# Taking the sparse steps out of the beats in which the gates are spread, and dividing the one-hots anew

## Chip, core and metric

The kernel runs on one core of a Trainium2 chip. The metric is the device time of one launch, in microseconds; before the change it is 4021.94 us, the median of three runs (4019.43 to 4031.22).

## The reference

A decoder trunk of two layers on 512 tokens of width 1024, all in float32. Each layer adds four mixers' outputs to the residual `h`, and then a product-key expert feed-forward; a last RMSNorm follows. The change touches the expert part alone:

```python
q = (xt @ wq).reshape(t, PEER_HEADS, 2, PEER_KEY_DIM)
sc = jnp.einsum('thcd,hcnd->thcn', q, keys)
s1, i1 = lax.top_k(sc[:, :, 0], PEER_TOPK)
s2, i2 = lax.top_k(sc[:, :, 1], PEER_TOPK)
...
top, pos = lax.top_k(cand, PEER_TOPK)
eidx = jnp.take_along_axis(cidx, pos, axis=-1)
gate = jax.nn.softmax(top, axis=-1)
...
act = jax.nn.gelu(jnp.einsum('td,tkd->tk', xb, u[ib]))
return jnp.einsum('tk,tkd->td', gb * act, v[ib])
```

Each token has 128 picks (8 heads of 16) out of 16384 experts. A pick costs a dot product with the expert's row of `u`, a GELU, a product with its gate, and the expert's row of `v` times that, added to the token.

## The kernel before, in words

Per layer the program runs the mixers, the output projection, then `peer`. `peer` normalises and transposes, computes the queries and ranks the keys, and calls `experts` (lines 1727 to 2004), which works on four chunks of 128 tokens in two ways at once.

**The sparse half.** Tokens 0 to 255 (chunks 0 and 1) gather their experts' rows. One step is one pick of 128 tokens. `gather(n)` on GpSimd (L1795) issues an indirect DMA that brings 128 rows of 2048 floats (a row of `u` and a row of `v`) into one of 7 slots. `dot(n)` on VectorE (L1958) multiplies the `u` half with the tokens and sums; ScalarE takes the GELU of two dots at a time (L1889); `add_row(m)` on VectorE (L1966, L1970), four steps behind (`LAG`), adds the `v` half times its coefficient to `h`. Gather n+3 is issued in the beat of step n and waits for add_row(n-4), which frees its slot. There are 256 steps in a layer.

**The dense half.** Tokens 256 to 511 (chunks 2 and 3) are multiplied with all experts, 128 tiles of 128. `with_u(j)` on TensorE (L1848) makes the tile's activations for 256 tokens, ScalarE takes the GELU (L1895), `gate_tile(j)` on VectorE (L1978) multiplies with the tile's gates, which are zero where a token did not pick the expert, and `with_v(j)` (L1859) adds the tile's output into four PSUM banks over all tiles. The `u` and `v` tiles are loaded by SyncE's queue through rings of four each (L1759, L1765). At most 22 activated tiles are held; 20 `u` tiles are run ahead.

**The gates of the dense half** have to be spread from (first key, second key, gate) triples to a table of 128 x 128 experts for each token. A quad is four tokens; there are 64. For each token one one-hot row over the first key carries the gate (`hot1`: iota equal to the pick, times the gate) and one over the second key does not (`hot2`). VectorE makes two of the four `hot1` of a quad (L1950), GpSimd the other two (L1805). ScalarE makes all four `hot2` with a Square for each (L1903) and one Relu over the four (L1907). TensorE multiplies `hot2` by `hot1` (`spread_quad`, L1837), ScalarE copies the result from PSUM (`copy_quad`, L1915), and after every fourth quad stores it to HBM (L1919). Both `hot` buffers and the PSUM banks are held for two quads, so the one-hots of quad q wait for the spread of quad q-2. After the last store SyncE loads the gates back, eight tiles at a time (L1770).

**The order** is written by hand in beats; each engine runs its own loop over the same 212 beats, and the engines meet only in semaphores. VectorE chooses the picks of chunk 0 before beat 0, and in 14 pieces each those of chunk 2 (from beat 0), chunk 3 (from beat 14) and chunk 1 (from beat 84): `choose_chunk`. Quad q is in beat 16+q, so quads fill beats 16 to 79. `u` tiles 0 to 19 are one in three beats up to beat 59. From beat 84 on (`TILES_AT`) each beat is one tile: `with_u` for tile 20 and on, and `gate_tile` and `with_v`. `steps_until(beat)` says how many sparse steps have been issued before a beat: one step in three beats, two in three after beat 28 (`chosen`), four in beats 80 to 83, and the rest evenly over the 128 tiles. Evaluated for the kernel before it gives 5 at beat 16, 43 at beat 80, 47 at beat 84 and 256 at the end: 1.633 steps a tile.

Of the kernel before, what the change touches and what calls it, by code (L numbers as in the profile page):

```python
# [17 lines left out]
ALU = mybir.AluOpType  # L18
# [43 lines left out]
@contextmanager  # L62
def stage(nc, *names):

    with ExitStack() as held:
        sems = {n: held.enter_context(nc.semaphore(n)) for n in names}
        with nc.Block() as block:  # L67
            yield block, sems
        for s in sems.values():
            nc.sync.sem_clear(s)  # L70
        nc.all_engine_barrier()
# [1446 lines left out]
CHOOSE_AT = {2: 0, 3: 14, 1: 84}  # L1518
PIECES = 14
# [3 lines left out]
QUADS_AT = 16  # L1523
TILES_AT = 84
# [2 lines left out]

def steps_until(beat):

    chosen = CHOOSE_AT[3] + PIECES  # L1530
    if beat <= TILES_AT - 4:
        return max(beat, 0) // 3 + max(beat - chosen, 0) // 3
    first = (TILES_AT - 4) // 3 + (TILES_AT - 4 - chosen) // 3 + 4
    if beat <= TILES_AT:
        return first + beat - TILES_AT
    return first + (min(beat, BEATS) - TILES_AT) * (STEPS - first) // TILES
# [14 lines left out]
def now(until, beat):  # L1551
    return range(until(beat), until(beat + 1))
# [174 lines left out]
def experts(nc, k, p, A, l):  # L1727

    with stage(nc, "dve_done", "shifted", "exps", "indexed", "chosen", "turned", "kept", "hot1", "hot1_pool", "squared", "hot2", "spread", "copied",
               "stored0", "stored1", "u_done", "gelus_u", "gated", "v_done", "dots", "gelus", "coefs", "summed", "y_added",
               "g_in0", "g_in1", *[f"u_in{n}" for n in range(U_RING)], *[f"v_in{n}" for n in range(V_RING)]) as (block, s):
        row_in = k.row_in
# [4 lines left out]
        spread = p.staging[:, :].rearrange("p (g j t) -> p g j t", g=2, j=P)  # L1739
# [4 lines left out]
        def act_of(j):  # L1744

            at = j % ACTS
            return own_acts[:, at, :] if at < OWN_ACTS else more_acts[:, at - OWN_ACTS, :]
# [39 lines left out]
        @block.gpsimd  # L1787
        def _(pool):
            def gather(n):
                t, pick = n // PICKS, n % PICKS  # L1790
                if pick == 0:
                    pool.wait_ge(s["indexed"], t + 1)
                if n >= ROW_SLOTS:
                    pool.wait_ge(s["summed"], n - ROW_SLOTS + 1)
                nc.gpsimd.indirect_dma_start(out=p.slots[:, n % ROW_SLOTS, :], out_offset=None, in_=A["peer_uv"],  # L1795
                                             in_offset=bass.IndirectOffsetOnAxis(ap=p.rows[:, t, pick:pick + 1], axis=0),
                                             ).then_inc(row_in[n % ROW_SLOTS], 16)

            def first_hots(q):
                if q % (QUADS // 2) == 0:  # L1800
                    pool.wait_ge(s["kept"], q // (QUADS // 2) + 1)
                if q >= 2:
                    pool.wait_ge(s["spread"], q - 1)
                for n in range(2, 4):
                    last = nc.gpsimd.tensor_scalar(p.hot1[:, 4 * (q % 2) + n, :], k.iota128[:, :], p.picks[:, 0, 4 * q + n:4 * q + n + 1],  # L1805
                                                   p.picks[:, 2, 4 * q + n:4 * q + n + 1], ALU.is_equal, ALU.mult)
                last.then_inc(s["hot1_pool"], 1)
            for n in range(ROW_SLOTS):
                gather(n)
            for beat in range(BEATS):  # L1810
                if 0 <= beat - QUADS_AT < QUADS:
                    first_hots(beat - QUADS_AT)
                for n in now(steps_until, beat):
                    if n >= LAG and n - LAG + ROW_SLOTS < STEPS:
                        gather(n - LAG + ROW_SLOTS)
            for n in range(ROW_SLOTS):
                pool.wait_ge(row_in[n], 16 * len(range(n, STEPS, ROW_SLOTS)))

        @block.tensor
        def _(pe):  # L1820
            def turn(t):
                pe.wait_ge(s["chosen"], ORDER.index(t) + 1)
                if t > SPARSE:
                    pe.wait_ge(s["kept"], t - SPARSE)
                for n in range(3):
                    last = nc.tensor.transpose(k.bank[4][:, n * P:(n + 1) * P], p.chosen[:, n, :], k.ident[:, :])
                last.then_inc(s["turned"], 1)

            def spread_quad(q):
                pe.wait_ge(s["hot1"], q + 1)  # L1830
                pe.wait_ge(s["hot1_pool"], q + 1)
                pe.wait_ge(s["hot2"], q + 1)
                if q >= 2:
                    pe.wait_ge(s["copied"], q - 1)
                for n in range(4):
                    at = 4 * (q % 2) + n
                    last = nc.tensor.matmul(k.bank[2 + q % 2][:, n * P:(n + 1) * P], p.hot2[:, at, :], p.hot1[:, at, :],  # L1837
                                            start=True, stop=True)
                last.then_inc(s["spread"], 1)

            def with_u(j):
                pe.wait_ge(u_in[j % U_RING], 16 * (j // U_RING + 1))
                if bank_before[j] is not None:
                    pe.wait_ge(s["gelus_u"], bank_before[j] + 1)
                elif bank_of[j] >= 2:
                    pe.wait_ge(s["copied"], QUADS)
                for b in range(DB):
                    last = nc.tensor.matmul(k.bank[bank_of[j]][:, 0:DENSE], u_raw[:, j % U_RING, b * P:(b + 1) * P], p.x_late[:, b, :],  # L1848
                                            start=b == 0, stop=b == DB - 1)
                last.then_inc(s["u_done"], 1)  # L1850

            def with_v(j):
                pe.wait_ge(v_in[j % V_RING], 16 * (j // V_RING + 1))
                pe.wait_ge(s["gated"], j + 1)
                if j == 0:
                    pe.wait_ge(s["kept"], 2)
                for t in range(2):
                    for half in range(2):
                        last = nc.tensor.matmul(k.bank[4 + 2 * t + half][:, :], act_of(j)[:, t * P:(t + 1) * P],  # L1859
                                                k.ring[:, j % V_RING, half * 512:(half + 1) * 512], start=j == 0, stop=j == TILES - 1)  # L1860
                last.then_inc(s["v_done"], 1)
            for beat in range(BEATS):
                for t in TURN_AT:
                    if beat == TURN_AT[t]:
                        turn(t)
                if 0 <= beat - QUADS_AT < QUADS:
                    spread_quad(beat - QUADS_AT)
                for j in now(u_until, beat):
                    with_u(j)
                if beat >= TILES_AT:  # L1870
                    with_v(beat - TILES_AT)

        @block.scalar
        def _(act):
# [21 lines left out]

            def second_hots(q):

                hot = p.hot2[:, 4 * (q % 2):4 * (q % 2) + 4, :]
                if q >= 2:  # L1900
                    act.wait_ge(s["spread"], q - 1)
                for n in range(4):
                    last = nc.scalar.activation(hot[:, n, :], k.iota128[:, :], ACT.Square, scale=-1.0,  # L1903
                                                bias=p.picks[:, 1, 4 * q + n:4 * q + n + 1])
                last.then_inc(s["squared"], 1)
                act.wait_ge(s["squared"], q + 1)
                nc.scalar.activation(hot, hot, ACT.Relu, scale=-1.0, bias=k.ones[:, 0:1]).then_inc(s["hot2"], 1)  # L1907
# [33 lines left out]
        def _(dve):  # L1941
            mark, settle = counted(dve, s["dve_done"])

            def first_hots(q):
                if q % (QUADS // 2) == 0:
                    dve.wait_ge(s["kept"], q // (QUADS // 2) + 1)
                if q >= 2:
                    dve.wait_ge(s["spread"], q - 1)
                for n in range(2):
                    last = nc.vector.tensor_scalar(p.hot1[:, 4 * (q % 2) + n, :], k.iota128[:, :], p.picks[:, 0, 4 * q + n:4 * q + n + 1],  # L1950
                                                   p.picks[:, 2, 4 * q + n:4 * q + n + 1], ALU.is_equal, ALU.mult)
                last.then_inc(s["hot1"], 1)
# [56 lines left out]
def peer(nc, k, A, l, gates):  # L2009
    with ExitStack() as held:  # L2010
# [35 lines left out]
        p.acts_u = sb("peer_acts_u", [P, OWN_ACTS * DENSE])  # L2046
        p.slots = sb("peer_slots", [P, ROW_SLOTS, 2 * DM])
        experts(nc, k, p, A, l)


# [103 lines left out]
```

## Time and profile before

| | us |
|---|---|
| median of three runs | 4021.94 |
| lowest and highest | 4019.43, 4031.22 |
| the profiled execution | 4015.8 |
| its span, first to last instruction | 4014.1 |
| TensorE busy | 3166.3 |
| VectorE busy | 2544.6 |
| GpSimd busy | 1102.9 |
| ScalarE busy | 933.6 |
| read from HBM, MB | 904.52 |
| mean granted clock of TensorE | 0.876 |

The span is that of the profiled execution; 1.7 us lie around it. Shares of busy time are means over stages with different limits, so the rows below are cut by stage. The expert part of the first layer runs from about 800 us to 2000 us, that of the second from about 2800 us to the end. A granted clock of 0.50 is 1.2 GHz, one of 1.00 is 2.4 GHz, and values between are a mix of the two over the stretch.

### The profile page before, as it was taken

How to read it: one execution, taken by the hardware profiler on the slowest of the kernel's cores; microseconds unless marked ns; L12 is line 12 of the kernel's file. 1: busy time of each engine (PE TensorE's matmuls, PEld its weight loads, DVE VectorE, ACT ScalarE, POOL GpSimd, SP SyncE). 2: the span in 40 equal slices, each digit the busy share in tenths (PEclk: the TensorE clock that was granted, in tenths of full speed). 3: DMA queues.
4: the chain of work that ended last, by engine and by line, in shares of the span. 5: the costliest groups of instructions: out<-in, count | busy, mean ns of one | idle time of the engine just before them, and what ended most of it. 6: DMA issues, size and time to landing. Idle time of an engine off the chain costs nothing. (4 is left out here: it accounts for less than half of the span.)

```text
span 4014.1 us, 39261 instructions
## 1 busy us (share of the span) xinstructions
PE 3166.3 (79%) x12836; PEld 2265.1 (56%) x12836; DVE 2544.6 (63%) x5150; ACT 933.6 (23%) x2020; POOL 1102.9 (27%) x1016
## 2 busy tenths in 40 slices
PE   6947677737689999999678477776476899999995
PEld 5725566636556665666266255665365566656662
DVE  3674544896686666666646645348966866666666
ACT  2331133137800000000033311231487000000000
POOL 0012111238922222222200121122498222222221
PEclk9969688868689999999889796888686999999997
DMA  3100112149899999999821001121498999999997
GB/s 103 49 0 1 46 34 82 58 143 317 288 356 411 417 416 417 417 416 406 320 94 37 0 1 46 43 79 58 173 320 284 366 415 417 417 417 417 413 403 303
DMA packets 235342, 943.29 MB, mean 235 GB/s; under 512 B 19584, under 2 KB 85632, under 8 KB 164864
## 3 DMA queue, kind: packets, MB, share of 16 engines
q0 software_dynamic: 73728, 536.90, 33.6%
q1 hardware_dynamic: 95360, 370.31, 24.1%
q10 hardware_dynamic: 66048, 33.56, 2.9%
q8 instruction: 102, 1.67, 0.2%
q14 instruction: 104, 0.85, 0.1%
HBM read 904.52 MB, written 35.65 MB: 234 GB/s over the span
## 5 line engine op out<-in xcount | busy, mean ns | idle before, releaser
L1848 PE MATMUL bank<-peer_x_late,xT 128*128 128x256 f32 x4096 | 987.3, 397 | 146.7 <-ACT peer_acts_u L1895 86.2
L1848 PEld LDWEIGHTS bank<-peer_x_late,xT 128*128 128x128 f32 x4096 | 818.3, 201 | 368.9 <-issue 174.6
L1795 POOL DMA_INDIRECT peer_slots<-in_peer_uv,peer_rows x512 | 542.3, 1059 | 1551.8 <-DVE h L1970 1412.7
L1958 DVE CUSTOM_DVE_ANT_0 peer_slots<-peer_slots,wide 128x1024 f32<-128x1024 f32 x512 | 627.4, 1225 | 512.7 <-DMA peer_slots<-in_peer_uv,peer_rows 511.7
L1970 DVE SCALAR_TENSOR_TENSOR h<-peer_slots,peer_coef,h 128x1024 f32<-128x1024 f32 x512 | 656.9, 1283 | 9.3
L1859 PE MATMUL bank<-ring,peer_acts_u 128*128 128x512 f32 x1344 | 616.9, 605 | 48.6 <-issue 33.3
L1859 PEld LDWEIGHTS bank<-ring,peer_acts_u 128*128 128x128 f32 x1344 | 259.8, 194 | 323.6 <-issue 301.6
L1805 POOL TENSOR_SCALAR peer_hot<-iota,peer_picks 128x128 f32<-128x128 f32 x256 | 329.6, 1294 | 23.7 <-PE bank L1837 20.7
L1837 PE MATMUL bank<-peer_hot 128*128 128x128 f32 x1024 | 195.7, 356 | 176.3 <-ACT peer_hot L1907 65.4
L1889 ACT ACTIVATE peer_coef<-peer_dots 128x2 f32<-128x2 f32 x256 | 51.2, 201 | 1201.1 <-DVE peer_dots L1958 1197.5
L1859 PE MATMUL bank<-ring,wide 128*128 128x512 f32 x704 | 321.1, 601 | 11.3 <-DVE wide L1978 9.9
L1837 PEld LDWEIGHTS bank<-peer_hot 128*128 128x128 f32 x1024 | 175.3, 257 | 195.8 <-issue 138.0
L1859 PEld LDWEIGHTS bank<-ring,wide 128*128 128x128 f32 x704 | 134.6, 192 | 153.5 <-issue 146.3
L1950 DVE TENSOR_SCALAR peer_hot<-iota,peer_picks 128x128 f32<-128x128 f32 x256 | 85.5, 384 | 142.7 <-PE bank L1837 142.0
L190 PE MATMUL bank<-mix_x_hi,w_hi 128*128 128x512 f32 x384 | 154.3, 402 | 12.6 <-DVE w_lo L280 12.6
L1903 ACT ACTIVATE peer_hot<-iota,peer_picks 128x128 f32<-128x128 f32 x512 | 161.9, 390 | 7.4 <-ACT peer_staging L1915 7.3
L1603 POOL TENSOR_TENSOR peer_w_lo<-ring,peer_w_hi 128x1024 fp32r<-128x1024 f32 x32 | 76.4, 2391 | 315.1 <-ACT peer_w_hi L1588 315.1
L191 PE MATMUL bank<-mix_x_lo,w_hi 128*128 128x512 f32 x384 | 153.0, 398 | 0.0
L192 PE MATMUL bank<-mix_x_hi,w_lo 128*128 128x512 f32 x384 | 152.9, 398 | 0.0
L1895 ACT ACTIVATE peer_acts_u<-bank 128x256 f32<-128x256 f32 x168 | 61.8, 378 | 365.9 <-PE bank L1848 363.4
L1915 ACT COPY peer_staging<-bank 128x512 f32<-128x512 f32 x128 | 131.5, 1027 | 57.4 <-PE bank L1837 51.1
L280 DVE TENSOR_TENSOR w_lo<-ring,w_hi 128x1024 fp32r<-128x1024 f32 x48 | 58.6, 1225 | 115.2 <-ACT w_hi L260 115.1
(449 smaller groups left out, 4190.0 us busy)
## 6 DMA issues: line engine op xcount, KB each, us to landing
xT<-in_peer_ut SPq DMA_DIRECT2D x256, 512.0 KB, 18.2
ring<-in_peer_uv SPq DMA_DIRECT2D x256, 512.0 KB, 18.3
gates<-peer_staging ACTq DMA_DIRECT2D x32, 1024.0 KB, 7.1
peer_staging<-gates SPq DMA_DIRECT2D x32, 1024.0 KB, 20.8
ring<-in_w_in SPq DMA_DIRECT2D x48, 512.0 KB, 3.5
ring<-in_peer_wq SPq DMA_DIRECT2D x32, 512.0 KB, 3.5
nsa_w<-in_cmp_w SPq DMA_DIRECT2D x2, 4096.0 KB, 12.1
ring<-in_w_out SPq DMA_DIRECT2D x16, 512.0 KB, 4.2
```

The source lines that it names most:

```text
L190: nc.tensor.matmul(out, left[0], right[0], start=first, stop=False)
L191: nc.tensor.matmul(out, left[0], right[1], start=False, stop=False)
L192: return nc.tensor.matmul(out, left[1], right[0], start=False, stop=last)
L1795: nc.gpsimd.indirect_dma_start(out=p.slots[:, n % ROW_SLOTS, :], out_offset=None, in_=A["peer_uv"], in_offset=bass.IndirectOffsetOnAxis(ap ...
L1805: last = nc.gpsimd.tensor_scalar(p.hot1[:, 4 * (q % 2) + n, :], k.iota128[:, :], p.picks[:, 0, 4 * q + n:4 * q + n + 1], p.picks[:, 2, 4 * ...
L1837: last = nc.tensor.matmul(k.bank[2 + q % 2][:, n * P:(n + 1) * P], p.hot2[:, at, :], p.hot1[:, at, :], start=True, stop=True)
L1848: last = nc.tensor.matmul(k.bank[bank_of[j]][:, 0:DENSE], u_raw[:, j % U_RING, b * P:(b + 1) * P], p.x_late[:, b, :], start=b == 0, stop=b ...
L1859: last = nc.tensor.matmul(k.bank[4 + 2 * t + half][:, :], act_of(j)[:, t * P:(t + 1) * P], k.ring[:, j % V_RING, half * 512:(half + 1) * 5 ...
L1903: last = nc.scalar.activation(hot[:, n, :], k.iota128[:, :], ACT.Square, scale=-1.0, bias=p.picks[:, 1, 4 * q + n:4 * q + n + 1])
L1915: nc.scalar.copy(spread[:, g % 2, :, at:at + 4].rearrange("p j t -> p t j"), k.bank[2 + q % 2][:, :].rearrange("p (t j) -> p t j", t=4)).t ...
L1958: nc.vector.tensor_tensor_reduce(out=u, in0=u, in1=k.wide[:, t, :], scale=1.0, scalar=0.0, op0=ALU.mult, op1=ALU.add, accum_out=p.dots[:, ...
L1970: nc.vector.scalar_tensor_tensor(out=k.h[:, t, :], in0=p.slots[:, m % ROW_SLOTS, DM:2 * DM], scalar=p.coef[:, t, pick:pick + 1], in1=k.h[: ...
```

## The change

```diff
 def steps_until(beat):
-    chosen = CHOOSE_AT[3] + PIECES
     if beat <= TILES_AT - 4:
-        return max(beat, 0) // 3 + max(beat - chosen, 0) // 3
-    first = (TILES_AT - 4) // 3 + (TILES_AT - 4 - chosen) // 3 + 4
+        return min(max(beat, 0), QUADS_AT) // 2
+    first = QUADS_AT // 2 + 4
     if beat <= TILES_AT:
         return first + beat - TILES_AT
     return first + (min(beat, BEATS) - TILES_AT) * (STEPS - first) // TILES
...
-            def first_hots(q):
+            def second_hots(q):
...
                 for n in range(2, 4):
-                    last = nc.gpsimd.tensor_scalar(p.hot1[:, 4 * (q % 2) + n, :], k.iota128[:, :], p.picks[:, 0, 4 * q + n:4 * q + n + 1],
-                                                   p.picks[:, 2, 4 * q + n:4 * q + n + 1], ALU.is_equal, ALU.mult)
-                last.then_inc(s["hot1_pool"], 1)
+                    last = nc.gpsimd.tensor_scalar(p.hot2[:, 4 * (q % 2) + n, :], k.iota128[:, :], p.picks[:, 1, 4 * q + n:4 * q + n + 1],
+                                                   None, ALU.is_equal)
+                last.then_inc(s["hot2_pool"], 1)
...
-                hot = p.hot2[:, 4 * (q % 2):4 * (q % 2) + 4, :]
+                hot = p.hot2[:, 4 * (q % 2):4 * (q % 2) + 2, :]
                 if q >= 2:
                     act.wait_ge(s["spread"], q - 1)
-                for n in range(4):
+                for n in range(2):
...
-                for n in range(2):
+                for n in range(4):
                     last = nc.vector.tensor_scalar(p.hot1[:, 4 * (q % 2) + n, :], k.iota128[:, :], p.picks[:, 0, 4 * q + n:4 * q + n + 1],
```

`steps_until` now gives 8 at beat 16, 8 at beat 80, 12 at beat 84 and 256 at the end: one step in two beats before the quads, none while the quads last, then four, and 1.906 steps a tile. VectorE makes all four `hot1` of a quad. Of the four `hot2`, ScalarE makes the first two (two Squares, and the Relu over 256 columns instead of 512) and GpSimd the last two, with one comparison instead of a comparison and a product. The counts of gathers, dots, additions, tiles and quads stay as they are, and so do the waits' places; `spread_quad` waits for `hot2_pool` where it waited for `hot1_pool`.

## Rows read from the trace of the kernel before

**Rows 1.** Windows, layer one: length, busy (instructions) by engine, clock, DMA

```profile
core 0: us, PE busy (x) PEld busy (x) DVE busy (x) ACT busy (x) POOL busy (x), PEclk, DMA share, GB/s
867.90:923.20 55.30, 41.09 (x184) 36.12 (x185) 46.16 (x95) 42.66 (x93) 39.79 (x31) 0.77 0.53 171
923.20:1037.50 114.30, 81.31 (x420) 72.32 (x419) 72.39 (x137) 92.34 (x210) 103.96 (x85) 0.85 0.96 330
1037.50:1104.40 66.90, 38.65 (x152) 33.90 (x153) 41.80 (x80) 52.31 (x116) 63.95 (x49) 0.50 0.82 269
1104.40:1126.80 22.40, 5.42 (x18) 4.17 (x17) 10.17 (x13) 1.45 (x3) 5.55 (x4) 0.65 1.00 355
1126.80:1230.00 103.20, 103.19 (x348) 67.02 (x349) 90.65 (x172) 8.67 (x27) 27.77 (x21) 0.98 0.94 368
1230.00:1800.00 570.00, 554.80 (x1901) 362.11 (x1900) 374.49 (x568) 37.04 (x148) 133.76 (x138) 0.99 1.02 416
...
1900.00:1950.00 50.00, 45.36 (x100) 19.58 (x99) 33.78 (x52) 1.24 (x7) 11.68 (x13) 0.93 1.00 401
```

**Rows 2.** Page, part 5: count, busy us, mean ns, idle before

```profile
L1958 DVE CUSTOM_DVE_ANT_0 peer_slots<-peer_slots,wide 128x1024 f32<-128x1024 f32 x512 | 627.4, 1225 | 512.7 <-DMA peer_slots<-in_peer_uv,peer_rows 511.7
L1970 DVE SCALAR_TENSOR_TENSOR h<-peer_slots,peer_coef,h 128x1024 f32<-128x1024 f32 x512 | 656.9, 1283 | 9.3
L1805 POOL TENSOR_SCALAR peer_hot<-iota,peer_picks 128x128 f32<-128x128 f32 x256 | 329.6, 1294 | 23.7 <-PE bank L1837 20.7
```

**Rows 3.** Timeline of POOL and DVE in the spread; start, length

```profile
1052.77 1.70 POOL L1805 TENSOR_SCALAR peer_hot<-iota,peer_picks 128x128 f32<-128x128 f32 x2
...
1053.27 0.60 DVE L1950 TENSOR_SCALAR peer_hot<-iota,peer_picks 128x128 f32<-128x128 f32 x2 [1.45 <-PE bank L1837]
...
1055.70 6.27 POOL L1805 TENSOR_SCALAR peer_hot<-iota,peer_picks 128x128 f32<-128x128 f32 x4
```

**Rows 4.** Timeline of ACT in the spread

```profile
1054.67 0.68 ACT L1903 ACTIVATE peer_hot<-iota,peer_picks 128x128 f32<-128x128 f32 x2
...
1058.60 1.26 ACT L1903 ACTIVATE peer_hot<-iota,peer_picks 128x128 f32<-128x128 f32 x4
1059.89 0.72 ACT L1907 ACTIVATE peer_hot<-peer_hot,ones 128x512 f32<-128x512 f32 x1
1060.52 1.03 ACT L1915 COPY peer_staging<-bank 128x512 f32<-128x512 f32 x1
```

**Rows 5.** Windows: PE and PEld on quads (L1837), then on u tiles (L1848)

```profile
923.20:1037.50 114.30, 39.56 (x256) 36.32 (x256) 0.85 0.96 330
...
923.20:1037.50 114.30, 45.36 (x161) 36.88 (x160) 0.85 0.96 330
```

**Rows 6.** Timeline of PE: quads, then the first tiles

```profile
1011.95 1.95 PE L1837 MATMUL bank<-peer_hot 128*128 128x128 f32 x16
...
1054.56 2.05 PE L1837 MATMUL bank<-peer_hot 128*128 128x128 f32 x8 [1.33 <-DVE peer_hot L1950]
...
1126.81 6.20 PE L1859 MATMUL bank<-ring,peer_acts_u 128*128 128x512 f32 x8 [16.99 <-issue]
1132.85 3.62 PE L1848 MATMUL bank<-peer_x_late,xT 128*128 128x256 f32 x16
```

**Rows 7.** Windows: DVE on one-hots (L1950) in the first quads

```profile
867.90:923.20 55.30, 8.93 (x28) 0.77 0.53 171
```

**Rows 8.** DMA queues and issues, page parts 3 and 6

```profile
q0 software_dynamic: 73728, 536.90, 33.6%
...
xT<-in_peer_ut SPq DMA_DIRECT2D x256, 512.0 KB, 18.2
...
peer_staging<-gates SPq DMA_DIRECT2D x32, 1024.0 KB, 20.8
```

**Rows 9.** Waits in the tile stage, 1230 to 1850 us

```profile
DVE peer_slots L1958 <- DMA peer_slots<-in_peer_uv,peer_rows: 199.0, 145, 4.3
```

**Rows 10.** Windows, tile stage of layer two, columns as in rows 1

```profile
3212.00:3840.00 628.00, 611.73 (x2098) 402.43 (x2097) 410.67 (x622) 41.04 (x164) 145.65 (x151) 0.99 1.02 416
```

More of the change, by code:

```diff
@@ L1727, in experts @@
 def experts(nc, k, p, A, l):
-    with stage(nc, "dve_done", "shifted", "exps", "indexed", "chosen", "turned", "kept", "hot1", "hot1_pool", "squared", "hot2", "spread", "copied",
+    with stage(nc, "dve_done", "shifted", "exps", "indexed", "chosen", "turned", "kept", "hot1", "hot2_pool", "squared", "hot2", "spread", "copied",
                "stored0", "stored1", "u_done", "gelus_u", "gated", "v_done", "dots", "gelus", "coefs", "summed", "y_added",
@@ L1811, in _ @@
                 if 0 <= beat - QUADS_AT < QUADS:
-                    first_hots(beat - QUADS_AT)
+                    second_hots(beat - QUADS_AT)
                 for n in now(steps_until, beat):
@@ L1830, in spread_quad @@
                 pe.wait_ge(s["hot1"], q + 1)
-                pe.wait_ge(s["hot1_pool"], q + 1)
+                pe.wait_ge(s["hot2_pool"], q + 1)
                 pe.wait_ge(s["hot2"], q + 1)
```

## The prediction

> **What bounds the kernel now.** I read the stages first, then the costliest groups, then the order of events inside a stage, then the transfers. The windows of layer one [rows 1] cut the expert part at the events that matter. From 867.9 to 1104.4 us the quads run, 236.5 us for 64. In the first 55.3 us (13 quads) VectorE is busy for 46.2, since it still chooses chunk 3's picks. In the next 114.3 us (32 quads, from the 256 matmul records at 8 a quad in [rows 5]) GpSimd is busy for 104.0 and ScalarE for 92.3. In the last 66.9 us (152 records, 19 quads) GpSimd is busy for 64.0, 96%: it is the bound, at 3.52 us a quad. From 1126.8 on the tiles run. There the DMA share is 1.02 at a flat 416 GB/s over 570 us, and TensorE is busy for 554.8 of them: both are full. Layer two repeats it [rows 10].
>
> Why GpSimd is slow can be read from two rows. A pair of its one-hots took 1.70 us where VectorE ran nothing beside it but one-hots; four took 6.27 us, 1.57 each, in a stretch that holds two dots and two row additions of VectorE [rows 3]. The mean over all is 1294 ns [rows 2]. So the sparse steps are what stretches GpSimd's work, and the change removes them from the quads.
>
> The transfers of a tile beat follow from sizes [rows 8]: a gather is 536.90 MB / 512 = 1.049 MB, a `u` and a `v` tile 0.524 MB each, an eighth of a gate load 0.131 MB. With 1.633 steps a beat that is 2.892 MB, at 416 GB/s 6.95 us.
>
> **The change part by part,** for one layer, on the profiled execution (4015.8 us; span 4014.1 and 1.7 around it). The median of the runs shown, 4021.94, lies 6 above.
>
> *Steps before the quads.* Eight instead of five by beat 16. VectorE is the engine that works towards the first quad there, and a step costs it 1.225 + 1.283 = 2.51 us [rows 2]. Three more: **+7.5**. Their gathers are ahead in the slots and cost nothing; without that cover each would cost a landing.
>
> *First 13 quads.* VectorE loses the five steps of beats 16 to 29, 12.6 us, and gains 26 one-hots at 8.93 / 28 = 0.32 us [rows 7], 8.3 us: 46.2 - 12.6 + 8.3 = 41.9 us busy. The choosing stays. I leave it 4 of its 9.1 us of waits: 46 instead of 55.3, **-9.3**.
>
> *The next 32 quads.* GpSimd: two one-hots at 0.85, 1.7 us, and no gathers among them. ScalarE: two Squares 0.68 instead of 1.26; the Relu over half the columns between 0.36 and the 0.72 of the full one, I take 0.50; the copy 1.03 [rows 4]. Sum 2.2 us. VectorE: four one-hots, 1.3 us. TensorE: quads and ten `u` tiles 39.6 + 45.4 us over 32 quads, 2.65 us each at the granted clock of 0.85 [rows 5]; with the clock at 1.00 it would be less, two quads then take 1.95 together and a `u` tile 3.62 [rows 6], (3 x 0.98 + 3.62) / 3 = 2.2. So the price lies between 2.2 and 2.65, or up to today's 3.57 (114.3 / 32) if the hand-overs hold it. I take 2.6, near the upper of the two busy sums, because ScalarE and TensorE wait for each other every second quad: 83.2 instead of 114.3, **-31.1**.
>
> *The last 19.* No `u` tiles. The clock was 0.50 here and a quad 2.05 us [rows 1, 6]. The loop over two quads is spread, copy, one-hots, spread: 2.05 + 1.03 + 0.68 + 0.50 and four hand-overs of about 0.12, 4.7 us, 2.37 a quad. I take 2.45: 46.6 instead of 66.9, **-20.3**. What is late next is ScalarE, no longer GpSimd.
>
> *The gap between the last quad and the first tile.* TensorE idles 17.0 us there, for the last store and the first gate load [rows 6], with the DMA engines full of gathers [rows 1]. Both steps of that path stay, the same four steps run beside it, but fewer transfers are under way. Between 0 and -8: **-3**.
>
> *The tiles.* Thirty-five steps arrive here (244 instead of 209). A beat now moves 1.049 + 0.131 + 1.906 x 1.049 = 3.179 MB, 7.64 us at 416 GB/s, so 128 x 0.69 = **+88**. At the 401 GB/s of 1900 to 1950 us [rows 1] it would be 92. VectorE pays 35 x 2.51 = 88 us too, and it has room: it is busy for 374.5 of 570 us and waits 199.0 us in 620 for gathers [rows 1, 9]; if that room were gone, its own beat would be 1.906 x 2.51, 4.8 us, and the gate product, still under 7.64. A gather on GpSimd's queue still waits only for `add_row`. Queued behind the later dots on VectorE are `gate_tile` and, through it, `with_v`; TensorE has 0.7 us a beat to give.
>
> Sum: 7.5 - 9.3 - 31.1 - 20.3 - 3 + 88 = **+32 us a layer, +64 in all**: 4080 for the profiled execution, and as the medians lie slightly above it, 4082. The reason in one line: a quarter of the quads' time is won, but the 36.7 MB that move had been riding in a stage with DMA room (330 and 269 GB/s) and now stand in one with none.
>
> **The rivals.**
>
> *The tile stage has room after all (the faster side).* If the transfers could go faster than the 416 GB/s because until now TensorE, 97% busy, held them back, the beat would stay at 6.95 us, and the sum would be 32 - 88 = -56 a layer, 3906. It decides at the beat at which the +88 shrinks to 56: 7.39 us, which needs 430 GB/s. For it: TensorE is full too. Against it: a DMA share of 1.02, 199 us of VectorE's waits for gathers, and 401 GB/s with the share still 1.00 in the window where TensorE has less to do. Chance 0.06. The Trainium skill (DMA: Bandwidth & Descriptors, Where 436 GB/s comes from) puts the ceiling of the sixteen engines at 435 GB/s. By that figure a beat would take 7.31 us, 46 us more a layer instead of 88, and the whole would come to about 4000; no row here shows more than 416.
>
> *The quads run at ScalarE's floor or a little under it.* Clock at 1.00, hand-overs hidden, Relu at 0.36: 51 quads at 2.0 are 102 instead of 129.8, the first 13 at 42: -32 a layer, back to about 4018, no change. Against it: both `hot` buffers tie the engines together within two quads. Chance 0.08.
>
> *VectorE's one-hots now block GpSimd.* If each of VectorE's four one-hots stopped GpSimd for its length, GpSimd would need 1.7 + 1.3 = 3.0 us a quad and stay the bound: 51 x 3.0 = 153 instead of 129.8, +23 a layer, 4128. The row speaks against it: the pair that took 1.70 us had 0.60 us of VectorE's one-hots inside its time [rows 3], and the same pair blocked would have shown 2.2 or more. The Trainium skill (SBUF — State Buffer, Who interferes with whom) states that a `tensor_scalar` of VectorE can enter a two-port mode and then holds GpSimd off for the whole instruction. By that rule this rival is what happens; the trace disagrees for this shape. Chance 0.08.
>
> *TensorE's clock.* At 0.50 in the middle stage too, three quads and a `u` tile take 3 x 2.05 + 2 x 3.62 = 13.4 us, 4.46 a quad, slower than today's 3.57: 32 x (4.46 - 2.6) = +60 a layer, 4200. A milder form has the gaps of a tenth of each tile beat lower the clock there; it binds when a beat's 6.8 us of TensorE work exceeds 7.64, so below a mean clock of 0.89. For it: 0.50 in the last quads. Against it: the engine gets busier in the quads, and between 1900 and 1950 us, with 9% idle, the clock is still 0.93 [rows 1]. Chance 0.10.
>
> That the steps do not move can't be: the schedule is counted out in the code.
>
> **How the numbers follow.** Forecast 0.68, clock 0.10, floor 0.08, blocked GpSimd 0.08, room in the tiles 0.06. About 0.3% (12 us) is what a measurement of this kernel can tell from no change. Faster: the room, 0.06. Same: the floor, 0.08. Slower: the rest, 0.86. The range takes the forecast's bounds, 51 quads at 2.2 (-18 a layer, 4047) and at 3.0 (+23, 4128), with a tile stage at 401 GB/s (+4 a layer, 4136), so it holds the blocked GpSimd and leaves out the floor, the room and most of the clock: 4040 to 4145.
>
> **What would show it.** The 64 quads should take about 176 us instead of 236.5, with GpSimd's one-hots near 0.82 us each and ScalarE the busiest of the helpers; DMA under 200 GB/s there. A tile beat should be about 7.6 us, at 416 GB/s, with TensorE near 90% busy. A DMA rate above 425 in the tiles, quads over 3 us, or a clock under 0.9 in the tiles would make the prediction wrong.

## The result and the profile after

The changed kernel takes 4133.74 us (median; 4126.31 to 4151.21) against 4021.43: the ratio is 1.0275, with a 95% interval of 1.0246 to 1.0305. Its profiled execution took 4126.31 us, 110.5 more than that of the kernel before. The stages of layer one, from the windows of the changed kernel (columns as in [rows 1]): the first 13 quads, the next 29, the last 22, the gap, and then stretches of the tile stage.

```profile
874.70:921.00 46.30, 35.39 (x177) 31.24 (x178) 38.81 (x102) 28.71 (x56) 20.13 (x26) 0.85 0.32 96
921.00:1003.00 82.00, 62.97 (x388) 57.15 (x386) 33.76 (x116) 61.31 (x128) 35.54 (x58) 0.98 0.61 183
1003.00:1052.80 49.80, 33.03 (x193) 29.27 (x194) 25.88 (x86) 43.01 (x87) 25.45 (x41) 0.86 0.41 117
...
1052.80:1076.90 24.10, 3.61 (x19) 2.88 (x17) 12.61 (x18) 1.46 (x3) 8.05 (x5) 0.64 0.84 301
1076.90:1180.00 103.10, 96.46 (x320) 60.65 (x320) 89.79 (x167) 7.84 (x24) 29.51 (x22) 0.99 0.96 373
...
1300.00:1400.00 100.00, 89.22 (x301) 55.78 (x300) 66.52 (x100) 6.19 (x26) 23.17 (x25) 1.00 1.02 417
...
1900.00:1950.00 50.00, 33.19 (x64) 13.45 (x63) 34.62 (x54) 2.04 (x9) 12.89 (x13) 0.86 0.97 373
1950.00:2000.00 50.00, 32.25 (x62) 12.48 (x60) 38.51 (x59) 1.63 (x8) 15.04 (x14) 0.90 0.98 367
2000.00:2050.00 50.00, 28.72 (x48) 11.04 (x48) 36.06 (x54) 1.22 (x6) 13.17 (x12) 0.82 0.87 316
```

The quads and the tiles as wholes, first of the kernel before, then of the changed one. The middle row of each three is the tile stage, from the first `with_v` to the last, the third its last 100 us.

```profile
867.90:1104.60 236.70, 161.25 (x756) 142.54 (x757) 160.35 (x312) 187.31 (x417) 207.88 (x164) 0.73 0.82 275
1126.80:1986.40 859.60, 830.18 (x2736) 524.08 (x2736) 590.77 (x928) 54.73 (x214) 209.24 (x205) 0.98 1.00 406
1886.40:1986.40 100.00, 87.22 (x193) 38.49 (x191) 70.57 (x108) 3.48 (x17) 27.22 (x26) 0.91 0.97 379
```

```profile
874.70:1053.00 178.30, 131.59 (x756) 117.85 (x757) 98.65 (x303) 133.03 (x269) 81.11 (x124) 0.91 0.48 142
1076.90:2043.10 966.20, 853.38 (x2736) 521.15 (x2736) 677.09 (x1050) 56.92 (x232) 240.70 (x240) 0.98 1.00 400
1943.10:2043.10 100.00, 67.38 (x120) 26.01 (x118) 74.83 (x113) 2.87 (x15) 30.08 (x28) 0.86 0.95 353
```

In layer one the first quad begins 6.8 us later (867.9 to 874.7), the quads take 58.4 less, the gap 1.7 more (22.2 to 23.9), the tiles 106.6 more: 57 us of the 110.4 by which the span grew. Layer two, cut in the same way, has quads of 236.5 and 179.1 us (57.4 less), gaps of 21.6 and 23.1 (1.5 more) and tiles of 859.9 and 957.1 (97.2 more). The rest of the growth lies ahead of its quads and behind its tiles.

The groups that answer to [rows 2] and [rows 3]: the page's line for GpSimd's one-hots, and one quad in the timeline.

```profile
L1804 POOL TENSOR_SCALAR peer_hot<-iota,peer_picks 128x128 f32<-128x128 f32 x256 | 167.0, 665 | 192.5 <-PE bank L1836 192.2
```

```profile
1031.06 1.17 DVE L1949 TENSOR_SCALAR peer_hot<-iota,peer_picks 128x128 f32<-128x128 f32 x4 [1.59 <-PE bank L1836]
1031.07 0.51 ACT L1906 ACTIVATE peer_hot<-peer_hot,ones 128x256 f32<-128x256 f32 x1
1031.12 1.27 POOL L1804 TENSOR_SCALAR peer_hot<-iota,peer_picks 128x128 f32<-128x128 f32 x2 [1.49 <-PE bank L1836]
```

GpSimd's mean fell from 1294 to 665 ns, and the engine that idled for 20.7 us behind TensorE's spreads now idles for 192.2. Its pair runs its 1.27 us right beside VectorE's four one-hots.

### The profile page after: what moved, and what is told of

Its sections match the earlier page's. It is cut to its first block and busy times, and to the rows that moved or that the text cites. A ratio compares the mean times of both kernels' runs of the same rounds, so it can differ in the third digit from the quotient of the medians.

```text
span 4124.5 us, 39267 instructions
## 1 busy us (share of the span) xinstructions
PE 3142.7 (76%) x12836; PEld 2201.6 (53%) x12836; DVE 2613.4 (63%) x5406; ACT 830.5 (20%) x1764; POOL 925.5 (22%) x1016
## 5 line engine op out<-in xcount | busy, mean ns | idle before, releaser
L1847 PE MATMUL bank<-peer_x_late,xT 128*128 128x256 f32 x4096 | 964.1, 390 | 202.9 <-ACT peer_acts_u L1894 159.5
L1847 PEld LDWEIGHTS bank<-peer_x_late,xT 128*128 128x128 f32 x4096 | 788.9, 195 | 442.0 <-issue 310.0
L1794 POOL DMA_INDIRECT peer_slots<-in_peer_uv,peer_rows x512 | 527.2, 1030 | 1669.8 <-DVE h L1969 1545.8
L1858 PE MATMUL bank<-ring,peer_acts_u 128*128 128x512 f32 x1344 | 633.3, 616 | 151.0 <-DVE peer_acts_u L1977 112.0
L1858 PEld LDWEIGHTS bank<-ring,peer_acts_u 128*128 128x128 f32 x1344 | 257.7, 197 | 452.1 <-issue 447.5
L1858 PE MATMUL bank<-ring,wide 128*128 128x512 f32 x704 | 323.4, 603 | 25.0 <-DVE wide L1977 24.9
L1836 PE MATMUL bank<-peer_hot 128*128 128x128 f32 x1024 | 156.0, 306 | 124.1 <-ACT peer_hot L1906 56.1
L1949 DVE TENSOR_SCALAR peer_hot<-iota,peer_picks 128x128 f32<-128x128 f32 x512 | 148.5, 357 | 158.7 <-PE bank L1836 157.7
L1858 PEld LDWEIGHTS bank<-ring,wide 128*128 128x128 f32 x704 | 135.4, 194 | 167.9 <-issue 164.0
L1836 PEld LDWEIGHTS bank<-peer_hot 128*128 128x128 f32 x1024 | 142.2, 214 | 138.8 <-DVE peer_hot L1949 98.7
L1804 POOL TENSOR_SCALAR peer_hot<-iota,peer_picks 128x128 f32<-128x128 f32 x256 | 167.0, 665 | 192.5 <-PE bank L1836 192.2
L190 PE MATMUL bank<-ffn_x_hi,peer_w_hi 128*128 128x512 f32 x256 | 103.8, 405 | 16.5 <-POOL peer_w_lo L1602 16.5
L191 PE MATMUL bank<-ffn_x_lo,peer_w_hi 128*128 128x512 f32 x256 | 101.2, 395 | 0.0
```

What stands on the lines that cost most here:

```text
L190: nc.tensor.matmul(out, left[0], right[0], start=first, stop=False)
L191: nc.tensor.matmul(out, left[0], right[1], start=False, stop=False)
L1804: last = nc.gpsimd.tensor_scalar(p.hot2[:, 4 * (q % 2) + n, :], k.iota128[:, :], p.picks[:, 1, 4 * q + n:4 * q + n + 1], None, ALU.is_equal)
```

## The experiments

Stage lengths are those of layer one, from windows cut as above. The moment of the first quad differs by up to 9 us between profiled executions of kernels with the same steps ahead of it, so lengths are compared and not times of day. Unless a row says otherwise, the order in a fence is quads, tiles.

### The two halves of the change apart

`hots_alone` is the changed kernel with the old `steps_until`; `steps_alone` is the kernel before with the new one.

> The new division of the one-hots with the old schedule of steps. Theory A (the sparse steps beside the quads are what stretches GpSimd's one-hots; the division saves only the shorter comparison and ScalarE's two Squares): the quads stay bound by GpSimd, its pair costs 1.27 us alone instead of 1.62 but is still stopped by the dots and additions, so 64 quads take 215 to 230 us instead of 236.5, the tile stage stays at 855 us, and the whole is 3985 to 4015. Rival B (ScalarE was the real bound of the quads, and the division does all of the 58 us a layer): quads near 180 us, the whole near 3910. Rival C (VectorE, now with four one-hots and two thirds of a step a quad, becomes the bound): quads at 236 us or more, 4020 or above.

Measured: 4004.74 us, ratio to the kernel before 0.9937 (0.9916 to 0.9958). Theory A: the quads and the whole lie in its ranges, and the tiles are 3 us above its 855. In layer two, though, the quads took 234.5 us, only 2.0 less than in the kernel before; why the two layers differ here is open.

```profile
868.30:1091.80 223.50, 154.25 (x756) 136.08 (x757) 196.15 (x438) 139.38 (x292) 166.05 (x163) 0.77 0.86 292
1115.60:1973.80 858.20, 828.76 (x2736) 526.05 (x2736) 589.81 (x926) 54.63 (x213) 206.21 (x205) 0.98 1.00 407
```

> The new schedule of steps with the old division of the one-hots. Theory A: GpSimd's pair falls to 0.81 us each, ScalarE at 2.9 to 3.1 us a quad is the bound; 64 quads take about 195 us (after: 178), the tile stage is as long as in the changed kernel (961 us), the whole 4160 to 4175. Rival B (the division does all of it): quads stay at 236 us, the whole near 4250.

Measured: 4232.73 us, ratio 1.0514 (1.0489 to 1.0539). The tile stage is as expected, the quads are not: 220.0 us (220.6 in layer two) where theory A said 195 and rival B 236, and so the whole is 58 us above A's range. GpSimd's one-hots came down as A said (888 ns in the mean, 791 at the median, 810 expected), but ScalarE's 2.9 to 3.1 us a quad did not turn out to be the price: it is 3.44.

```profile
874.40:1094.40 220.00, 161.26 (x756) 142.80 (x757) 67.77 (x179) 181.13 (x392) 110.92 (x125) 0.74 0.39 115
1117.00:2082.20 965.20, 853.21 (x2736) 523.26 (x2736) 676.25 (x1048) 56.89 (x231) 244.92 (x240) 0.97 0.99 399
```

So the quads of layer one gain 13 us by the division alone, 17 by the schedule alone and 58 by both; those of layer two gain 2, 16 and 57. Before, GpSimd was busy for 208 of 237 us and ScalarE for 187: two engines near their limit. Freeing GpSimd alone (111 of 220) leaves ScalarE with 181 of 220; relieving ScalarE alone (139 of 223.5) leaves GpSimd's one-hots stretched, at 985 ns, and loads VectorE to 196. TensorE shows the same: its mean clock in the quads is 0.73, 0.77 and 0.74 in these three, and 0.91 with both, where a repeating pattern of three quads and a `u` tile takes 8.13 us with short gaps:

```profile
926.95 1.13 PE L1836 MATMUL bank<-peer_hot 128*128 128x128 f32 x8 [1.96 <-ACT peer_hot L1906]
927.91 3.62 PE L1847 MATMUL bank<-peer_x_late,xT 128*128 128x256 f32 x16
931.37 1.95 PE L1836 MATMUL bank<-peer_hot 128*128 128x128 f32 x16
935.08 1.13 PE L1836 MATMUL bank<-peer_hot 128*128 128x128 f32 x8 [1.77 <-POOL peer_hot L1804]
```

The mean clock moved together with the waits, and which drives which is not shown: how much of the interplay (28 us in layer one, some 39 in layer two) is the clock and how much the waits was not taken apart.

### Gathers in flight: LAG 3

```diff
-LAG = 4
+LAG = 3
```

> The changed kernel with LAG 3 instead of 4: a row is added three steps after its dot, so its slot is free one step earlier and four gathers are under way instead of three. Theory D (the 18 us a layer beyond the transfers' price are the last 20 tiles, where u loads have ended and three gathers in flight can't fill the DMA engines: 373, 367 and 316 GB/s): the DMA rate after 1900 us rises to about 400, the middle of the tile stage stays at 416 and 7.6 us a beat, and the whole falls by 20 to 36 us to 4098 to 4114. Rival E (the excess is the clock or VectorE's own work): no change, 4125 to 4140, or slower if VectorE waits for the GELU.

> The kernel before with LAG 3. Theory D: its tail already ran at 401 GB/s, so there is less to win, 0 to 10 us in all: 4010 to 4022. Rival E: no difference or slower. A gain as large as that of the changed kernel (20 us or more) would say that gathers in flight limit the whole tile stage and not just the tail.

Measured: the changed kernel 4097.12 us (ratio to the kernel before 1.018, 1.0154 to 1.0207), the kernel before 4010.11 (0.9965, 0.9951 to 0.998). Tile stage and its last 100 us, changed kernel, then the kernel before, both with LAG 3:

```profile
1086.60:2026.60 940.00, 863.02 (x2736) 527.88 (x2736) 677.16 (x1051) 58.88 (x232) 251.41 (x239) 0.96 1.01 410
1926.60:2026.60 100.00, 78.51 (x165) 32.42 (x163) 79.15 (x121) 3.05 (x15) 34.40 (x29) 0.93 1.00 405
```

```profile
1135.60:1988.00 852.40, 831.20 (x2736) 521.44 (x2736) 590.22 (x928) 55.32 (x214) 245.22 (x204) 0.99 1.01 409
1888.00:1988.00 100.00, 90.51 (x212) 41.80 (x210) 75.32 (x116) 3.48 (x17) 27.44 (x27) 0.93 1.00 406
```

The tail fills as theory D said: with a fourth gather under way the last 100 us move 405 GB/s instead of 353, and the tiles of the two kernels differ by 940.0 - 852.4 = 87.6 us (88.2 in layer two), the 88 of the prediction. The whole is 1 us below D's range, and the kernel before gains little, as expected. But gathers in flight are only a part of the reason. Who waited for whom in the tile stage, from 1850 us on in the changed kernel, and from 1800 in the kernel before:

```profile
PE bank L1858 <- DVE peer_acts_u L1977: 36.8, 12, 5.7
PE bank L1858 <- DVE wide L1977: 12.0, 4, 4.2
```

```profile
PE bank L1859 <- DVE wide L1978: 4.9, 2, 3.7
...
PE bank L1859 <- DVE peer_acts_u L1978: 3.2, 1, 3.2
```

And how many tiles VectorE had gated (L1978, L1977) and TensorE multiplied with `v` (L1859, L1858, eight records a tile) by 1800 us: the kernel before, the changed kernel, the changed kernel with LAG 3. Behind the length stand the busy time and records of VectorE, or of TensorE and its weight loads, then clock, DMA share and GB/s.

```profile
1050.00:1800.00 750.00, 41.73 (x100) 0.94 0.99 397
1050.00:1800.00 750.00, 341.48 (x752) 142.84 (x752) 0.94 0.99 397
```

```profile
1050.00:1800.00 750.00, 39.55 (x95) 0.98 1.00 403
1050.00:1800.00 750.00, 343.62 (x758) 143.10 (x759) 0.98 1.00 403
```

```profile
1050.00:1800.00 750.00, 40.03 (x96) 0.95 0.99 402
1050.00:1800.00 750.00, 333.97 (x730) 136.92 (x731) 0.95 0.99 402
```

The kernel before has gated 100 tiles and multiplied 94. So six tiles lie ready, and at the end, when the `u` loads have ceased, TensorE works them off and `v` loads keep coming beside the gathers. In the changed kernel it is 95 and 95: VectorE, waiting for gathers, is the slower side, TensorE waits for each tile's gates, and in the last 100 us it gets through 15 tiles where the kernel before does 22. LAG 3 brought the lead back, 96 and 91. So there it did two things at once. In the kernel before, which had its lead already, the fourth gather alone took the tail from 379 to 406 GB/s (layer two: 389 to 404); in the changed kernel both together took it from 353 to 405 (372 to 400). About half of the change is then left for the lead, by difference only: four gathers without a lead were not run.

### The price of a moved step, and whether a better place exists

Four kernels are `hots_alone` with LAG 3 and differ in `steps_until` up to beat 80: the old schedule (`hots_lag3`, 47 steps by beat 84); one in three all through (`third_lag3`, 30); one in two from beat 28 (`half_lag3`, 39); and the old one with a step in every beat from 60 on (`more_lag3`, 53):

```diff
# third_lag3
-        return max(beat, 0) // 3 + max(beat - chosen, 0) // 3
+        return max(beat, 0) // 3
# half_lag3
+        return min(max(beat, 0), chosen) // 3 + max(beat - chosen, 0) // 2
# more_lag3
+        return max(beat, 0) // 3 + max(beat - chosen, 0) // 3 + max(beat - 60, 0) // 3
```

> The new division of the one-hots, the old schedule of steps, and LAG 3: the two parts that gained by themselves. If they are independent (quads 236.5 to 223; tail filled), the gains of 0.63% and 0.35% add up: 3985 to 3995. If both worked on the same wait, no better than 4000 to 4005.

> As hots_lag3, with one step in three beats all through the quads: 30 steps instead of 47 by beat 84, so 17 go to the tile stage. Theory F (a moved step costs the transfer of its rows, 2.52 us, in the tile stage, and brings back less in the quads): tile stage +43 us (852 to 895), quads from 223 to between 190 and 200, whole +20 to +40 over hots_lag3. Rival G (the quads' gain is all had by halving the steps, since GpSimd then is no longer the bound): quads near 180, the tile stage +43, whole within 5 us of hots_lag3.

> hots_lag3 with one step in two beats instead of two in three from beat 28: 39 steps by beat 84 instead of 47. Theory F with what third_lag3 showed (17 steps moved: tiles +42, quads and gap -38 a layer): between the two, tiles +20, quads and gap -18 to -24, the whole 3992 to 4004.

> As hots_lag3, with a step in every beat of the last 20 quads: 53 steps instead of 47 by beat 84. Theory F: tile stage -15 us a layer (852 to 837), the last 20 quads bound by VectorE at 1.2 + 2.5 = 3.7 to 3.9 us a quad instead of about 3.4, +6 to +10 us; the whole 10 to 18 us below hots_lag3. Rival: in the quads gathers come too late (three or four in flight and 1.03 us of GpSimd each), the quads grow by 15 us or more and nothing is won.

| kernel | steps by beat 84 | quads | gap | tiles | median us | ratio to before |
|---|---|---|---|---|---|---|
| `more_lag3` | 53 | 245.9 | 24.0 | 840.5 | 4003.41 | 0.9934 (0.9911 to 0.9957) |
| `hots_lag3` | 47 | 225.8 | 24.0 | 852.4 | 3999.41 | 0.9928 (0.9906 to 0.995) |
| `half_lag3` | 39 | 206.0 | 27.2 | 872.2 | 4002.27 | 0.995 (0.9929 to 0.997) |
| `third_lag3` | 30 | 193.3 | 18.9 | 894.6 | 4007.36 | 0.9953 (0.9935 to 0.997) |
| `after_lag3` | 12 | 180.9 | 24.8 | 940.0 | 4097.12 | 1.018 (1.0154 to 1.0207) |

The two ends as windows, `third_lag3` and then `more_lag3`:

```profile
877.60:1070.90 193.30, 140.83 (x756) 126.28 (x757) 152.69 (x375) 137.28 (x282) 104.41 (x145) 0.83 0.76 245
1089.80:1984.40 894.60, 844.25 (x2736) 526.01 (x2736) 633.14 (x988) 56.58 (x223) 233.02 (x221) 0.97 1.01 412
```

```profile
876.90:1122.80 245.90, 152.54 (x756) 134.67 (x757) 213.32 (x463) 139.58 (x294) 172.61 (x170) 0.74 0.85 290
1146.80:1987.30 840.50, 821.59 (x2736) 521.62 (x2736) 577.45 (x910) 54.83 (x211) 221.81 (x198) 0.99 1.01 408
```

The medians come from three sessions, in which the kernel before took 4024.05, 4027.99 and 4025.32 us, so the ratios compare better than they do. From 47 steps down to 12 the tile stage is a straight line: 8 steps cost 19.8 us, 17 cost 42.2, 35 cost 87.6, about 2.5 each, the time of 1.049 MB at 416 GB/s. The quads are no line. The first 17 steps taken out bring 32.5 us, the next 18 only 12.4: no engine is busy for more than 79% of `third_lag3`'s quads, so what holds them by then is likely the hand-overs of the two-quad loop, which no run takes apart. The change went past the point where a step is worth moving. Theory F's price was right; its "+20 to +40" for `third_lag3` was too dark, it is +8 on the medians, while the quads, 193.3, lie in F's range and not near rival G's 180. `half_lag3` came out as expected in the tiles and the whole, and `more_lag3` won nothing since the quads grew by 20 us where 6 to 10 were expected. Between 30 and 53 steps the whole is nearly flat, and the intervals overlap. `hots_lag3` has the lowest median, and `hots_alone`, 0.9937, can't be told from it: LAG 3 and the division did not add up to the 3985 to 3995 hoped for.

### The gap, and GpSimd's share

`after_no_four` is the changed kernel without the four steps of beats 80 to 83.

```diff
-    first = QUADS_AT // 2 + 4
+    first = QUADS_AT // 2
     if beat <= TILES_AT:
-        return first + beat - TILES_AT
+        return first
```

> The changed kernel without the four steps of beats 80 to 83; they go to the tile stage. Theory H (the gap between quads and tiles is the last store and the first gate load queueing behind these steps' gathers, 15 us for a store that alone takes 5.5): the gap falls from 24 to 12 to 15 us, the tile stage grows by 4 x 2.52 = 10 us, the whole stays within 10 us of 4125 to 4134. Rival (the gap is latency of its own): the gap stays at 22 to 24, the whole grows by 20 us.

Measured: 4137.37 us, ratio 1.0278 (1.0249 to 1.0307), no different from the changed kernel. The gap is 14.1 us instead of 23.9, the tiles 970.2 instead of 966.2 (layer two: 12.7 for 23.1, 974.9 for 957.1). The last store and SyncE's first gate load after it, in the changed kernel and then here:

```profile
1054.08 0.52 ACTq L1918 DMA_DIRECT2D gates<-peer_staging  x1
...
1069.13 0.81 SPq L1769 DMA_DIRECT2D peer_staging<-gates  x2
```

```profile
1055.19 0.52 ACTq L1918 DMA_DIRECT2D gates<-peer_staging  x1
...
1061.03 0.81 SPq L1769 DMA_DIRECT2D peer_staging<-gates  x2
```

Theory H: 15.1 us from store to load with the steps' gathers beside it, 5.8 without. The gap is filled with useful transfers, so closing it won nothing.

Three kernels give GpSimd three of the `hot2` and ScalarE one (shown for the changed kernel).

```diff
-                for n in range(2, 4):
+                for n in range(1, 4):
...
-                hot = p.hot2[:, 4 * (q % 2):4 * (q % 2) + 2, :]
+                hot = p.hot2[:, 4 * (q % 2):4 * (q % 2) + 1, :]
-                for n in range(2):
+                for n in range(1):
```

> The changed kernel with one hot2 of a quad on ScalarE and three on GpSimd. Theory I (the quads of the changed kernel are bound by ScalarE, busy for 97 of 123 us after the first 13 quads): ScalarE loses a Square and half the Relu, 0.4 us of its 2.2 a quad, GpSimd goes from 1.27 to 1.9 us; quads from 178 to 160 to 168, the whole 4100 to 4115. Rival J (the two-quad loop binds, whoever is in it): GpSimd's three one-hots in a row, 1.9 us, are now as long as ScalarE's copy, Square and Relu, and the quads stay at 175 or more, the whole at 4120 to 4140.

> third_lag3 with the same division (ScalarE one, GpSimd three). Theory I: quads from 193 to about 180, the whole 10 to 25 us below third_lag3's 4007. Rival J: within 5 us of it, or slower as the steps now stop GpSimd for longer.

> half_lag3 with ScalarE one and GpSimd three of the hot2. Theory I: quads 5 to 12 us shorter than half_lag3's. Rival J: GpSimd, stopped by the steps beside it, becomes the bound again and the quads grow by 5 us or more.

Measured: `after_pool3` 4122.61 us (1.025, 1.0222 to 1.0279), quads 170.6 instead of 178.3; `third_pool3` 4041.75 (1.0061, 1.0041 to 1.008), quads 207.0 instead of 193.3; `half_pool3` 4043.77 (1.0061, 1.0043 to 1.008), quads 225.8 instead of 206.0. Quads of `after_pool3`, then of `half_pool3`:

```profile
883.90:1054.50 170.60, 132.09 (x756) 117.78 (x757) 99.91 (x303) 109.07 (x206) 120.64 (x187) 0.91 0.51 148
```

```profile
873.40:1099.20 225.80, 155.27 (x756) 135.89 (x757) 184.93 (x408) 113.77 (x224) 194.82 (x216) 0.76 0.75 247
```

Without steps ScalarE was a part of the bound: relieving it by 24 us of work gave 7.7 (10.9 in layer two), which lies between theories I (quads of 160 to 168) and J (175 or more). The whole, at 1.025, can't be told from the changed kernel's 1.0275. With steps beside the quads the same move costs 14 and 20 us, and GpSimd is busy for 86% of them. Its one-hots take 664 ns each in the mean without steps, 814 and 872 with them. Steps alone don't do that: in `third_lag3` the mean of the pair is 653 ns, in `half_lag3` 808. What matters is when a one-hot starts. Here are single instructions, one of `third_lag3` and then one of `hots_alone`, each with the dot beside it:

```profile
1004.34 0.60 POOL L1805 TENSOR_SCALAR peer_hot<-iota,peer_picks 128x128 f32<-128x128 f32 x1
...
1004.70 1.21 DVE L1958 CUSTOM_DVE_ANT_0 peer_slots<-peer_slots,wide 128x1024 f32<-128x1024 f32 x1
```

```profile
922.29 1.21 DVE L1958 CUSTOM_DVE_ANT_0 peer_slots<-peer_slots,wide 128x1024 f32<-128x1024 f32 x1
922.59 1.39 POOL L1805 TENSOR_SCALAR peer_hot<-iota,peer_picks 128x128 f32<-128x128 f32 x1
```

The one-hot that began before the dot took 0.60 us, as with nothing beside it; the one that began 0.30 us after the dot took 1.39. In `third_lag3` none of the 256 begins inside a dot or a row addition. With three in a row (`third_pool3`) 46 of 384 do, and 24 more begin less than 0.1 us before a dot and are held too, at 1.66 us: the 88 that overlap a dot or an addition take 1.39 us in the mean, the other 296 take 0.64. That shows that the steps hold up GpSimd's one-hots. That it is the whole of the 14 and 20 us is not shown, since TensorE's clock fell as well (0.83 to 0.80, and 0.80 to 0.76).

## Why the prediction was right, and where a size was off

The direction, the mechanism and the range held: 4133.7 lies in 4040 to 4145. The growth was 110 us where the sum said 64, and most of the 46 between is one term, the tiles.

- **Steps before the quads.** +7.5 forecast, +6.8 measured, against a scatter of some us between executions (`after_pool3`, with the same steps, begins its quads 9 us later still).
- **The quads.** -60.7 forecast, -58.4 measured (-57.4 in layer two). The match of the sum is in part luck, for two misses offset each other: the 29 quads in the middle took 6.6 us more than their price, the last 22 took 4.6 less. By thirds: 13 quads in 46.3 us (46 forecast); 2.83 us a quad in the 29 after them (2.6); 2.26 in the last 22 (2.45), where TensorE's clock was 0.86 and not the 0.50 taken. The Relu took 0.51 (0.50). GpSimd's one-hots took 0.665 us and not the 0.82 named as a sign: the 0.85 had been read from the form with a product.
- **The gap.** -3 forecast, +1.7 measured. Its wait is for the four steps' gathers (`after_no_four`), which are the same as before; that fewer other transfers run brought nothing.
- **The tiles.** "+88" was the mis-sized term: 106.6 measured, and 97.2 in layer two. The 88 is what 35 transfers cost in a full stage, and with LAG 3 in both kernels it is what is measured, 87.6. The prediction applied 0.69 us to all 128 beats as if the stage stayed full to its end, and named 401 GB/s as the worst. With LAG 4 the last 100 us ran at 353 GB/s (372 in layer two), with three gathers in flight and no gated tiles in hand. Against 416 that is 15 us lost where the kernel before lost 9 (379), and the 60 us ahead of it, at 370 GB/s, lose 7 more; the rest was not traced. The text named the queue (`with_v` behind `gate_tile`, behind the dots) but priced it at nothing because of 0.7 us of room in a beat. What the queue cost was VectorE's lead of six tiles, and the lead showed its worth only at the end.
- **Rival, room in the tile stage.** Excluded: 418 GB/s is the most that the stretches of the stage show with 35 more gathers. The 435 GB/s of the Trainium skill (DMA: Bandwidth & Descriptors, Where 436 GB/s comes from) was not reached in any run.
- **Rival, VectorE's one-hots block GpSimd.** Excluded: the pair took 1.27 us beside 1.17 us of them and 1.21 where nothing ran beside it (`third_lag3`, at 1000.52 us). By the rule of the Trainium skill (SBUF — State Buffer, Who interferes with whom) for a `tensor_scalar` in a two-port mode the pair would have taken some 2.4; this shape doesn't do it. What the same section says of VectorE instructions with two SBUF inputs, that they contend with a GpSimd instruction that reads SBUF, fits: the dots and row additions have two, and the one-hots that overlap them in `third_pool3` took 1.39 us in the mean where the others took 0.64.
- **Rival, TensorE's clock.** It rose in the quads, 0.73 to 0.91, and stayed at 0.98 over the tiles. In the last 100 us of them it was 0.86 (0.91 before), with TensorE busy for 67 of them and waiting for gates.
- **Rival, the floor.** The quads did not reach 42 + 102 us; 178.3 is 34 above it.

## What to carry to other kernels

Work that is taken out of a slow stage has to be paid for where it goes, and the price there is that of the full resource: here 2.5 us of transfer for each step, known beforehand from bytes and a flat 416 GB/s. What it brings falls off as soon as the next engine binds (32 us for the first 17 steps, 12 for the next 18), so a schedule is better moved in parts than all at once. A stage that is full in its middle need not be full at its end: count the transfers in flight when one of the streams stops, and count in the trace which engine still has a backlog.

## What was not expected of the hardware

Two small gains on engines that hand over to each other, 13 and 17 us in layer one and 2 and 16 in layer two, made 58 and 57 together. TensorE's granted clock went with it: 0.73 to 0.77 in the quads with one of the two changes or none, 0.91 with both. A one-hot of GpSimd that starts before a dot of VectorE takes 0.60 us, one that starts 0.30 us after it 1.39, so the same steps cost two one-hots a quad nothing (`third_lag3`, 653 ns) and three in a row much (`third_pool3`, 814). And GpSimd's one-hot with a single comparison takes 0.602 us at the median, where the one with comparison and product never took less than 0.780.
